# Sliding-window scores: the low-part products of a head pair as two 64-row matmuls in one layer kernel

## The reference

```python
def swa_sinks_attention(q, k, v, sinks):
    ...
    k_band = jnp.concatenate([jnp.pad(kb[:, :-1], pad), kb], axis=2)
    v_band = jnp.concatenate([jnp.pad(vb[:, :-1], pad), vb], axis=2)
    sc = jnp.einsum('bntkgd,bnskd->bnkgts', qb, k_band,
                    preferred_element_type=jnp.float32) * scale
    ...
    sc = jnp.where(mask[None, :, None, None], sc, NEG_INF)
    ...
    p = jax.nn.softmax(jnp.concatenate([sc, sink], axis=-1), axis=-1)[..., :-1]
    o = jnp.einsum('bnkgts,bnskd->bntkgd', p.astype(v.dtype), v_band)
```

## Time and profile before

| | |
|---|---|
| median of 3 runs | 1784.22 us (1783.39 to 1784.88) |
| the profiled execution | 1783.47 us |
| its span, first to last instruction | 1781.7 us |
| TensorE busy | 1745.5 us, 98% of the span |
| DVE busy | 1190.4 us, 67% |
| ACT busy | 813.5 us, 46% |
| steps of B | 4 units of 8, from about 1085 to 1512 us |

### The profile page before, as it was taken

One profiled execution on the slowest core, in us unless ns is written; L12 is line 12 of the kernel. 1 busy time (PEld: TensorE's weight loads), 2 busy tenths in 40 slices (PEclk: granted clock), 3 DMA queues, 4 the chain that ended last, 5 costly groups with the idle time before them and its releaser, 6 DMA issues.

```text
span 1781.7 us, 28435 instructions
## 1 busy us (share of the span) xinstructions
PE 1745.5 (98%) x8904; PEld 1470.9 (83%) x8904; DVE 1190.4 (67%) x2409; ACT 813.5 (46%) x2154; POOL 450.0 (25%) x668
## 2 busy tenths in 40 slices
PE   6999999999999999999999999999999988999999
PEld 6978888888888888888888888888888867778887
DVE  6742675866757767677676675876868788436764
ACT  5411445544544545454454544444544565333321
POOL 3231221412313223132131222422424334100000
PEclk9999999999999999999999999999999999999999
DMA  6222333433433333433334334453433666587665
GB/s 236 67 77 83 114 116 123 123 113 94 133 122 99 122 106 122 128 104 101 120 123 131 104 105 127 140 162 112 140 101 109 193 209 194 175 274 238 212 197 171
DMA packets 278091, 245.82 MB, mean 138 GB/s; under 512 B 32112, under 2 KB 220528, under 8 KB 276848
## 3 DMA queue, kind: packets, MB, share of 16 engines
q1 hardware_dynamic: 278000, 244.68, 43.8%
HBM read 174.35 MB, written 70.25 MB: 137 GB/s over the span
## 4 chain that ended last, share of the span: by engine, by line
PE 89%; DVE 3%; ACT 1%; DMA 0%; issue 0%; SPq 0%; DVEq 0%; ACTq 0%
PE ps_a L1048 22%; PE ps_a L1050 22%; PE ps_a L1049 22%; PE ps_b L1139 3%; PE ps_a L1099 3%; PE ps_b L1154 3%; PE ps_a L1098 2%; PE ps_b L1048 2%; PE ps_b L1049 2%; PE ps_b L1050 2%; PE ps_b L1092 2%; PE ps_b L1185 1%; PE ps_b L1156 1%; DVE w_lo_sb L1347 1%; PE ps_b L1168 1%; PE ps_b L1167 1%
## 5 line engine op out<-in xcount | busy, mean ns | idle before, releaser
L1048 PE MATMUL ps_a<-hT_hi,w_hi_sb 128*128 128x512 f32 x1600 | 651.8, 407 | 6.2 <-DVE w_lo_sb L1347 3.2
L1050 PE MATMUL ps_a<-hT_hi,w_lo_sb 128*128 128x512 f32 x1600 | 627.1, 392 | 0.0
L1049 PE MATMUL ps_a<-hT_lo,w_hi_sb 128*128 128x512 f32 x1600 | 624.3, 390 | 0.0
L1050 PEld LDWEIGHTS ps_a<-hT_hi,w_lo_sb 128*128 128x128 f32 x1600 | 300.5, 188 | 66.9
L1048 PEld LDWEIGHTS ps_a<-hT_hi,w_hi_sb 128*128 128x128 f32 x1600 | 301.1, 188 | 65.9 <-DVE w_lo_sb L1347 6.9
L1049 PEld LDWEIGHTS ps_a<-hT_lo,w_hi_sb 128*128 128x128 f32 x1600 | 301.9, 189 | 54.7
L1347 DVE TENSOR_TENSOR w_lo_sb<-w_raw_sb,w_hi_sb 128x512 fp32r<-128x512 f32 x305 | 230.2, 756 | 172.9 <-ACT w_hi_sb L819 171.3
L819 ACT ACTIVATE w_hi_sb<-w_raw_sb 128x512 fp32r<-128x512 f32 x304 | 189.9, 626 | 189.8 <-PE ps_a L1050 52.8
L1347 DVE TENSOR_TENSOR ps_a<-ps_a,mask 128x128 f32<-128x128 f32 (+2 forms) x192 | 77.8, 419 | 200.6 <-PE ps_a L1099 200.0
L937 ACT ACTIVATE attention_parts<-ps_b 128x512 fp32r<-128x512 f32 (+3 forms) x160 | 76.9, 521 | 213.3 <-PE ps_b L1139 213.2
L1018 ACT ACTIVATE expd<-ps_a,neg_max 128x256 f32<-128x256 f32 (+7 forms) x128 | 95.1, 743 | 158.3 <-DVE neg_max L1577 155.8
(11 more groups left out here) (147 smaller groups left out, 2840.3 us busy)
## 6 DMA issues: line engine op xcount, KB each, us to landing
w_raw_sb<-in_w_in SPq DMA_DIRECT2D x192, 256.0 KB, 3.0
w_out_sums<-in_w_out SPq DMA_DIRECT2D x64, 256.0 KB, 3.9
w_out_sums_dram<-w_out_sums SPq DMA_DIRECT2D x64, 256.0 KB, 2.8
w_raw_sb<-w_out_sums_dram SPq DMA_DIRECT2D x64, 256.0 KB, 3.0
qkv_a_dram<-stage_rows SPq DMA_DIRECT2D x48, 256.0 KB, 2.5
qkv_sb<-qkv_a_dram SPq DMA_DIRECT2D x64, 192.0 KB, 2.9
w_out_sums<-y_dram SPq DMA_DIRECT2D x24, 512.0 KB, 4.9
w_raw_sb<-in_w_out SPq DMA_DIRECT2D x48, 256.0 KB, 3.7
```

The source lines that it names most:

```text
L1048: pe.matmul(dst, a_hi, b_hi, start=start, stop=False)
L1049: pe.matmul(dst, a_hi, b_lo, start=False, stop=False)
L1050: return pe.matmul(dst, a_lo, b_hi, start=False, stop=stop)
```

## The change

In `scores_b` the loops are turned round: p outside, r inside. For each p, the two products with the high part of the keys (r = 0 and 1) come first, over 128 partitions as before. Then come the two products with the low part of the keys, each over 64 partitions alone: the upper half for r = 0, the lower half for r = 1, which are the halves that hold the high part of the queries. The product of the two low parts is left out thereby. The number of matmuls stays at eight for a step. `s_done` is still incremented twice, now by the last two matmuls of the step.

```diff
-                for r in range(2):
-                    for p in range(2):
-                        mm = q_times_k(p_s[:, r, p * 256 + lo:p * 256 + 256],
-                                       q_pair[:, (2 * r + p) * P:(2 * r + p + 1) * P], k_dup[0][:, t], kT_lo[0][:, t])
-                    mm.then_inc(sm["s_done"], 1)
+                for p in range(2):
+                    c = slice(p * 256 + lo, p * 256 + 256)
+                    for r in range(2):
+                        q = slice((2 * r + p) * P, (2 * r + p + 1) * P)
+                        pe.matmul(p_s[:, r, c], q_pair[:, q], k_dup[0][:, t], start=True, stop=False)
+                    for r, h in enumerate(half_rows):
+
+                        q = slice((2 * r + p) * P, (2 * r + p + 1) * P)
+                        mm = pe.matmul(p_s[:, r, c], q_pair[h, q], kT_lo[0][h, t], start=False, stop=True)
+                        if p:
+                            mm.then_inc(sm["s_done"], 1)
```

## The result

The changed kernel takes 1799.77 us (median of 4 runs, 1798.42 to 1800.99), the kernel before 1784.24 us beside it. The ratio is 1.009, with a 95% interval from 1.0078 to 1.0102: slower by 15.5 us in the medians (16.1 us, 13.9 to 18.2, by the ratio). Forecast were 6.0 us more and a range up to 1797.5 us. The sign was right, the size was not.

The account below looks back on a forecast made before the run. TensorE was taken to bound units 8 to 10, a DVE and ACT chain unit 11. Form changes less saved places, 3.9 us, plus later masks, 2.1 us, gave 6.0 us more: 1784.2 to 1790.2 us, range 1778.5 to 1797.5 us.

Parts of the forecast that it names:

- What bounds the kernel: TensorE's work counts in full in units 8 to 10, hardly in unit 11, where waits run through DVE and ACT.
- What the change takes away: Score matmuls: low products pair up, eight queue places become six per step, 5.7 us saved in units 8 to 10.
- What it adds: TensorE, each step: four changes between 128 and 64 rows at 0.10 us, 9.6 us over 24 steps.
- both one after the other: At a form change: wait for a matmul's end, then unhidden weight load, 0.26 us; total 1808.0 us, chance 0.08.
- my own sum: Whole kernel: 3.9 us in units 8 to 10 plus 2.1 us for unit 11's masks, 6.0 us more.
- its two cases together: TensorE drains at form changes: end waited for, 0.16 us (1796.9 us, chance 0.14), or with load, 0.26 us (1808.0 us, 0.08).
- What it moves: First s_done increment, and so DVE's mask, 0.54 us later; hidden in units 8 to 10, costing 2.1 us in unit 11.
- My sum for unit 11: Mask delay in full at steps 2, 3 and 7, partly at 4 and 6, none at 5: 2.1 us.
- A wait that I had ruled out: Units 8 to 10: no wait on TensorE was expected; one appearing would show the prediction wrong.
- cover at the probabilities: Units 8 to 10: probabilities are scaled 4.5 us before TensorE asks for them, against a mask delay of 0.54 us.
- The rivals: Other outcomes: faster 0.24; small change price 0.18; pairs one behind the other 0.08; end waited for 0.14, with load 0.08.
- The faster case: Form changes free, each pair takes one place, only the later increment costs: 5.0 us less, 1779.3 us, chance 0.24.

Follow-up runs that it names:

- one product: Kernel before with only the last low product of each step (r = 1, p = 1) over 64 rows, order unchanged: 1790.61 us, ratio 1.0044.
- two changes: Changed kernel's eight matmuls reordered against the kernel before, both 64-row pairs adjacent, full products around them: 1788.74 us, ratio 1.0041.
- eight: Kernel before in its old order, each low product alone over 64 rows, so eight form changes per step: 1822.79 us, ratio 1.0226.
- The order alone: Kernel before with only the new order and later increments, all eight products still over 128 rows: 1785.59 us, ratio 1.0014.
- the change by unit: Two kernels, the change applied against the kernel before only in units 8 to 10 (1796.80 us, 1.0078) or only in unit 11 (1786.60 us, 1.0020).
- all on one half: Four adjacent 64-row products per step, all on the upper half, output altered, against the kernel before: 1797.16 us, ratio 1.0080.
- the kernels by half: Four adjacent 64-row products, both of r = 0 then both of r = 1, against the kernel before: 1789.10 us; with separate source lines 1790.07 us.

## Why the prediction was wrong

**What bounds the kernel: right.** A microsecond of TensorE counts in units 8 to 10 and hardly in unit 11: the change in unit 11 alone cost 3.6 us, where 7 us would have been due in full.

**What the change takes away: right.** Two places of 0.119 us in each step; four products on one half against four on two give 0.22 us back.

**What it adds: this is the step that failed, by the size of its term.** The price of one change of form was put at 0.10 us; measured are 0.17 (one product), 0.183 (the change), 0.19 (two changes, and eight). The bounds from 0 to 0.26 us held it. I chose the end that was "a measured distance", the unhidden weight load, as if it were the whole. It is one of two parts. The other is a wait before the load may start: 0.20 to 0.21 us from the start of the last matmul of the old form, instead of 0.119 to the next matmul, so 0.09 us. 0.09 + 0.10 = 0.19 us. I had this case too, "both one after the other", but took the wait from the modelled end of a matmul (0.283 us), and so got 0.26 us for it and gave it 0.08. The end of a matmul in this view is modelled, and the distances show the next form begin 0.07 us sooner. With 0.183 us my own sum gives 24 x (0.73 - 0.24), less 0.5 for the steps of 128 columns, = 11.3 us, and for the masks 3 x 0.79 + (0.79 - 0.35) + (0.79 - 0.29) = 3.3 us, 14.6 us, and the waits in units 8 to 10 make it 15.8: within the interval of the measured time (13.9 to 18.2 us more).

The Trainium skill's page "TensorEngine Tiling (Array Packing)", Key Properties, had said that a change of the tiling mode drains TensorE. The traces agree with it as far as they go: each change has 0.09 us of wait ahead of it and a weight load that isn't pulled ahead, 0.10 us. I had weighed this rule as a rival, with 0.22 for its two cases together, and the measured price lies between the two, nearer to the first.

**What it moves: right in kind.** The mask was to start 0.54 us later and starts 0.82 us later, which is the two places and three changes of 0.19. Steps 2, 3 and 6 pay as forecast. Step 4 pays 0.08 us where 0.46 were due with this delay, and step 5 pays 0.71 us where I had none. My sum for unit 11 with the measured price, 3.3 us, meets the measured 3.3 us by luck: steps 4 and 5 are wrong by -0.4 and +0.7 us, the 0.8 us of step 7 lie behind where the columns end, and 0.3 of the measured 3.3 us lie between steps 0 and 1 and are no work of the new scores, as the kernel with the old scores in unit 11 has them too (0.4 us).

**A wait that I had ruled out.** "If a wait on TensorE appears in these units, where I expect none": it does, three times for the gate, 0.9 us in all, and once, 0.3 us, for the last output of A. My list of waits had none for the gate, but the timeline of before has 0.10 us of it in step 5 of each unit, hidden in the list behind a modelled end: the place had no cover to begin with. I had looked for cover at the probabilities (4.5 us) and not followed DVE's queue to the end of the half step, where the gate stands behind some 7 us of work without a gap (1163.15 to 1170.21 us in the one shown). The order alone shows it: 1.5 us in units 8 to 10 with TensorE's steps unchanged. The mask comes 0.82 us later there and TensorE 0.5 us, and the difference, 0.3 us, is the wait that each gate adds.

**The rivals.** The faster case needed a price under 0.015 us; the pairs did go side by side, their two starts 3 to 4 ns apart, and it wasn't enough. The kernel with two changes is the best that was tried of this idea: 0.39 us for two changes, 0.24 saved.

Open: which part of the array's work the 0.09 us stand for. With 128 columns a pair is followed by the next full product after 1206.11 - 1205.85 = 0.26 us, with 256 after 0.31, 0.05 us for 128 columns. That is half of what 256 columns more cost in a full queue (0.12 us from start to start with 256 columns, 0.22 to 0.23 with 512). So the wait grows with the columns as the pace of long matmuls does, and what is left of it doesn't depend on them:

```profile
1205.85 0.33 PE L1128 MATMUL ps_a<-attention_parts,q_hi_lo 64*128 64x128 f32 x2
1206.11 0.44 PE L1124 MATMUL ps_a<-attention_parts,q_hi_lo 128*128 128x128 f32 x2
```

That this rest is the time to empty the array fits, but no run here separates it. The two parts of the change by unit add up: 12.5 + 3.6 = 16.1 us in the spans, where the change has 16.2 (in the runs 17.5 us against 16.1, within the intervals).

## What to carry to other kernels

Count how often a stream of matmuls changes between row forms before counting what side by side saves: here a change cost 0.17 to 0.19 us and a saved matmul of 256 columns gave 0.12, so two changes need about three saved places between them to break even. Put all 64-row products of a step together, and where there are too few of them, use all 128 rows, as the kernel before does. And when a reordering moves a semaphore, follow the waiting engine's queue as far as it runs without a gap; the piece that hurts may be the last one in it. A place without a listed wait isn't a place with cover: TensorE waited 0.10 us for the gate where the list had nothing.

## What was new about the hardware

- A change between 128-row and 64-row matmuls, in either direction, costs 0.19 us with 256 columns (0.14 with 128): 0.09 us of wait, and 0.10 us of weight load that is issued together with its matmul instead of one matmul ahead. In front of the transposes the load's part is 0.06 us instead of 0.10; why isn't shown.
- 64-row matmuls on different halves start within 0.01 us of each other (lines 1130 and 1132), and within one half they keep the pace of 0.12 us from start to start (all on one half). They don't keep the program's order across the halves: the third started 0.21 us ahead of the second (lines 1130 to 1133). The Trainium skill's page "TensorE: Matmul & The Clock Gate", Part 3, says that matmuls start and end in the order of the program; on this trace the starts did not, and the measurement decides. The ends shown don't keep it either (1115.53 us for the third, 1115.64 for the second), but these are modelled. In the kernels by half no wait hung on it, since the increments sit on full products behind; in the changed kernel they sit on a pair, whose two products start in the order of the program.
- TensorE's share of busy time stayed at 98% while it lost 11 us in such seams, of 1797. Distances between starts show them, shares don't.
